# Forget block with heads in pairs, decay rows added by VectorE, and attention half steps between the products; projection after the gate in the PLE blocks

## What is computed

```python
def fox_mixer(hn, w_in, b_f, g_qn, g_kn, w_o):
    z = hn @ w_in                      # q, k, v: 16 heads of 64 each, and 16 forget logits
    log_f = jax.nn.log_sigmoid(f_logit + b_f)
    decay = jnp.cumsum(log_f, axis=1)
    q = rms_norm(q, g_qn)
    k = rms_norm(k, g_kn)
    # softmax over s <= t of q.k / 8 + decay[t] - decay[s], times v
    o = block_causal_attention(q, k, v, decay)
    return o.reshape(b, s, hd) @ w_o
# PLE, at the end of each layer
gate = jax.nn.sigmoid(rms_norm(h, g_ple[i]) @ ple_w_gate[i])
h = h + gate * (p[i] @ ple_w_proj[i])
```

## Time and profile before

| what | value |
|---|---|
| median of three runs | 1390.44 us |
| the profiled execution, own time | 1387.38 us |
| its span | 1385.6 us |
| TensorE busy | 1342.7 us, 97% |
| VectorE busy | 796.2 us, 57% |
| ScalarE busy | 676.5 us, 49% |

### The profile page before, as it was taken

How to read it: one execution, slowest core, us unless ns; L and a number is a source line. 1 busy time by engine, 2 the same in 40 slices (tenths; PEclk the granted TensorE clock), 3 DMA queues, 4 the chain that set the end, 5 groups by cost and what they waited for, 6 DMA issues and landing times.

```text
span 1385.6 us, 17642 instructions
## 1 busy us (share of the span) xinstructions
PE 1342.7 (97%) x6539; PEld 1110.8 (80%) x6539; DVE 796.2 (57%) x1008; ACT 676.5 (49%) x949; POOL 145.9 (11%) x206
## 2 busy tenths in 40 slices
PE   8999998899999999999999999999999899999996
PEld 6888787778888887888888878888888687888875
DVE  6655548784555546655545566555554645654664
ACT  6444336655444437544435463544444635447441
POOL 1000003611000001000001400000000142110500
PEclk9999999899999999999999999999999999999999
DMA  9655535234655654555553442465564478544531
GB/s 302 197 183 188 193 138 158 87 108 152 200 186 189 213 182 153 180 184 182 195 188 135 162 142 70 130 197 188 183 213 152 152 201 262 160 145 159 188 138 31
DMA packets 148526, 234.35 MB, mean 169 GB/s; under 512 B 10103, under 2 KB 103447, under 8 KB 148208
## 3 DMA queue, kind: packets, MB, share of 16 engines
q1 hardware_dynamic: 143680, 222.52, 49.4%
q0 software_dynamic: 4480, 10.85, 2.7%
q10 hardware_dynamic: 304, 0.14, 0.0%
HBM read 231.33 MB, written 4.49 MB: 170 GB/s over the span
## 4 chain that ended last, share of the span: by engine, by line
PE 84%; DVE 6%; ACT 3%; DMA 3%; issue 2%; POOL 1%; SPq 0%; POOLq 0%; DVEq 0%; ACTq 0%
PE acc L541 17%; PE acc L543 17%; PE acc L542 16%; PE acc L574 9%; PE acc L575 8%; PE acc L578 8%; PE misc L616 4%; DMA raw<-in_w_in_dram 2%; DVE wl L1474 1%; ACT xh L1095 1%; ACT wh L1059 1%; DVE xl L1500 1%; PE acc L754 1%; DMA rstd_by_token<-rstd 1%; PE misc L771 1%
## 5 line engine op out<-in xcount | busy, mean ns | idle before, releaser
L1474 DVE TENSOR_TENSOR wl<-raw,wh 128x2048 fp32r<-128x2048 f32 (+2 forms) x206 | 466.1, 2269 | 266.8 <-ACT wh L1059 266.5
L1059 ACT ACTIVATE wh<-raw 128x2048 fp32r<-128x2048 f32 (+2 forms) x206 | 387.4, 1888 | 174.4 <-PE acc L578 152.9
L541 PE MATMUL acc<-wh,xh 128*128 128x512 f32 (+2 forms) x848 | 333.4, 393 | 5.3 <-DVE wl L1474 2.7
L543 PE MATMUL acc<-wh,xl 128*128 128x512 f32 (+2 forms) x848 | 328.3, 387 | 0.0
L542 PE MATMUL acc<-wl,xh 128*128 128x512 f32 (+2 forms) x848 | 327.9, 387 | 0.0
L541 PEld LDWEIGHTS acc<-wh,xh 128*128 128x128 f32 x848 | 160.2, 189 | 39.2 <-issue 4.3
L543 PEld LDWEIGHTS acc<-wh,xl 128*128 128x128 f32 x848 | 160.1, 189 | 32.9
L542 PEld LDWEIGHTS acc<-wl,xh 128*128 128x128 f32 x848 | 160.5, 189 | 30.6
L574 PE MATMUL acc<-wh,ah 128*128 128x512 f32 x320 | 125.7, 393 | 0.0
L575 PE MATMUL acc<-wl,ah 128*128 128x512 f32 x320 | 124.6, 389 | 0.0
L2063 POOL TENSOR_SCALAR rstd<-ssq 128x1 f32<-128x1 f32 x20 | 10.3, 516 | 928.1 <-ACT hn L1079 927.8
(11 more groups left out here) (298 smaller groups left out, 1712.4 us busy)
## 6 DMA issues: line engine op xcount, KB each, us to landing
raw<-in_ffn_w_in_dram SPq DMA_DIRECT2D x172, 512.0 KB, 4.7
raw<-in_ffn_w_out_dram SPq DMA_DIRECT2D x88, 512.0 KB, 4.4
raw<-in_w_in_dram SPq DMA_DIRECT2D x64, 512.0 KB, 4.8
raw<-in_fox_w_in_dram SPq DMA_DIRECT2D x24, 512.0 KB, 4.2
raw<-in_ple_w_gate_dram SPq DMA_DIRECT2D x16, 512.0 KB, 4.1
raw<-in_mla_w_o_dram SPq DMA_DIRECT2D x8, 512.0 KB, 4.0
raw<-in_fox_w_o_dram SPq DMA_DIRECT2D x8, 512.0 KB, 4.5
raw<-in_w_out_dram SPq DMA_DIRECT2D x8, 512.0 KB, 4.7
```

The costliest lines, as they stand in the source:

```text
L541: pe.matmul(dst, hi, rhs_h, start=first, stop=False)
L543: return pe.matmul(dst, lo, rhs_h, start=False, stop=last)
L1059: act.activation(wh[:, s, 0:n], raw[:, s, 0:n], ACT.Copy).then_inc(hi_done, 1)
L1474: dve.tensor_tensor(wl[:, s, 0:n], raw[:, s, 0:n], wh[:, s, 0:n].bitcast(F32), ALU.subtract)\
```

## The change

In the forget block:
- Heads go in eight pairs. q and k of a pair are turned together, without the extra columns; the scores of the two heads are products of 64 rows at partitions 0 and 64, in different banks.
- The decay isn't in the product any more. TensorE turns the negated sums to rows, GpSimd writes them to DRAM and reads them back for all partitions (`negc`, 2 MB), and adds the causal mask (`mask_decay`). VectorE adds them to the scores with tensor_tensor_reduce, which gives the maximum too.
- Chunks come in the order q, k, v, q, k, v, so pairs 0 to 3 are ready after half of the projection. The pipeline of a pair is in half steps (even: turn q and k, products with v of two pairs before, turn the result, which ScalarE rounds and VectorE takes the remainder of; odd: scores, turn the probabilities of the pair before). Half steps 0 to 8 stand behind half groups of the projection (`FOX_AT`), the others between the products of the output matrix (`o_rows`), which begin as soon as a pair's result is turned.
- ScalarE and VectorE follow the same order; each now copies one lane of the turned probabilities.

In the PLE blocks the gate comes first and the projection after it; `pp` is gone, VectorE multiplies the gate by the accumulator; before the last block the roundings alternate between the token tiles and both squares stand behind them. Its core:

```diff
+PAIRS = H // 2
+FOX_CHUNKS = [0, 2, 4, 1, 3, 5]
+FOX_TURN = {4: (0, 1), 5: (2,), 6: (3,), 7: (4,), 8: (5,), 9: (6,), 10: (7,)}
+FOX_AT = {(7, 1): (0,), (8, 0): (1,), (8, 1): (2,), (9, 0): (3,), (9, 1): (4,), (10, 0): (5,), (10, 1): (6,),
+          (11, 0): (7,), (12, 1): (8,)}
+FOX_REST = 9
...
-                wide(g, I["ple_w_proj"][i], 0)
                 for k in range(4):
-                    wide(g + 1 + k, I["ple_w_gate"][i], 256 * k)
+                    wide(g + k, I["ple_w_gate"][i], 256 * k)
+                wide(g + 4, I["ple_w_proj"][i], 0)
...
+                def gate_wait(t, k):
+                    if t == 0 and k == DK - 2:
+                        rows_ready(pe, r, 1)
+                        turn_rows(nname, 1)
+                    ready(t, k)
+                wide_stage(g, q, xh, xl, DK, 0, gate_wait, None, True)
...
+                    for n in range(2):
+                        open_tile(q + 2 + n, t)
+                        for k in range(2):
+                            if t + n + k == 3:
+                                turn_h(after, r_after)()
+                            mm = products(acc(q + 2 + n, t), ph[:, k, t * P:(t + 1) * P], pl[:, k, t * P:(t + 1) * P],
+                                          wh[:, s, w], wl[:, s, w], k == 0, k == 1)
+                        mm.then_inc(acc_ready if t == 0 else (proj_ready, w_used)[n], 1)
...
+            def even(i):
+                if i < PAIRS:
+                    fill = q + fox_fill(1 if i < PAIRS // 2 else 4)
+                    if i % (PAIRS // 2) == 0:
+                        pe.wait_ge(acc_read[fill % 2], acc_reads(fill))
+                    for b, src in enumerate((qf, kf)):
+                        open_m(b, hr[b] + 2 * i)
+                        for t in range(NT):
+                            mm = turn(b, slice(t * P, (t + 1) * P), src[:, t, i * P:(i + 1) * P])
+                        mm.then_inc(m_ready[b], 1)
+                j = i - 2
+                if 0 <= j < PAIRS:
+                    fill = q + fox_fill(2 if j < PAIRS // 2 else 5)
+                    if j % (PAIRS // 2) == 0:
+                        pe.wait_ge(acc_read[fill % 2], acc_reads(fill))
+                    pe.wait_ge(m_read[2], hr[2] + 2 * j + 1)
+                    pe.wait_ge(m_read[3], hr[3] + probs_at(j) + 1)
+                    for lane in range(2):
+                        v = vf[:, :, (2 * j + lane) * HD:(2 * j + lane + 1) * HD]
+                        for t, blocks in enumerate((((0, 0),), ((1, 0), (2, 1)))):
+                            for n, (col, kt) in enumerate(blocks):
+                                mm = pe.matmul(M[:, 2, t * P + lane * HD:t * P + (lane + 1) * HD],
+                                               pTf[:, lane, col * P:(col + 1) * P], v[:, kt, :],
+                                               start=n == 0, stop=n == len(blocks) - 1)
+                    mm.then_inc(m_ready[2], 1)
+                if i in FOX_TURN:
+                    open_m(3, hr[3] + turned_at(i))
+                    for n, j in enumerate(FOX_TURN[i]):
+                        pe.wait_ge(m_read[2], hr[2] + 2 * j + 2)
+                        for t in range(NT):
+                            mm = turn(3, slice(n * S + t * P, n * S + (t + 1) * P), hn[:, t, j * P:(j + 1) * P])
+                    mm.then_inc(m_ready[3], 1)
+            def odd(i):
+                if i < PAIRS:
+                    for b in range(2):
+                        pe.wait_ge(m_read[b], hr[b] + 2 * i + 1)
+                    for t, w in enumerate((P, S)):
+                        for lane in range(2):
+                            rows = slice(lane * HD, (lane + 1) * HD)
+                            mm = pe.matmul(M[:, lane, t * P:t * P + w], qTf[rows, t * P:(t + 1) * P], kTf[rows, 0:w],
+                                           start=True, stop=True)
+                            if t:
+                                mm.then_inc(m_ready[lane], 1)
+                j = i - 1
+                if 0 <= j < PAIRS:
+                    for lane in range(2):
+                        pe.wait_ge(fox_exp, 2 * j + lane + 1)
+                        open_m(2 + lane, hr[2 + lane] + (2 * j, probs_at(j))[lane])
+                        for n in range(3):
+                            mm = turn(2 + lane, slice(n * P, (n + 1) * P), prf[:, j % 2, lane, n * P:(n + 1) * P])
+                        mm.then_inc(m_ready[2 + lane], 1)
...
+            for n in range(1, 6):
+                fill = q + fox_fill(n)
+                open_acc(fill)
                 for k in range(2):
...
+                    w = fox_group(n) + k
+                    wait_group(g + w)
+                    for half in range(2):
+                        for j in range(2 * half, 2 * half + 2):
+                            for t in range(NT):
+                                cols, wc = slice(t * P, (t + 1) * P), slice(512 * j, 512 * j + 512)
+                                mm = products(acc(fill, t), xh[:, 4 * k + j, cols], xl[:, 4 * k + j, cols],
+                                              wh[:, (g + w) % RING, wc], wl[:, (g + w) % RING, wc],
+                                              k + j == 0, k == 1 and j == 3)
+                                if t == 0 and k == 1 and j == 3:
+                                    mm.then_inc(acc_ready, 1)
+                        if half:
+                            mm.then_inc(w_used, 1)
+                        attend((w, half))
...
+            def o_rows(j, t):
+                s = (g + 13 + j // 2) % RING
+                if t == 0 or j < 5:
+                    wait_group(g + 13 + j // 2)
+                    e = min(i for i in FOX_TURN if j in FOX_TURN[i])
+                    pe.wait_ge(m_read[3], hr[3] + turned_at(e) + 1)
+                for n in range(2):
+                    if j == 0:
+                        open_tile(q + 7 + n, t)
+                    w = slice((j % 2) * D + n * 512, (j % 2) * D + (n + 1) * 512)
+                    mm = products(acc(q + 7 + n, t), xh[:, j, t * P:(t + 1) * P], xl[:, j, t * P:(t + 1) * P],
+                                  wh[:, s, w], wl[:, s, w], j == 0, j == DK - 1)
+                    if j == DK - 1 and t == 0:
+                        mm.then_inc(acc_ready, 1)
+                if t == NT - 1 and j % 2:
+                    mm.then_inc(w_used, 1)
+            for n in range(FOX_REST, 2 * PAIRS + 3):
+                (odd if n % 2 else even)(n // 2)
+                if n >= 10:
+                    o_rows((n - 10) // 2, (n - 10) % 2)
+            o_rows(4, 1)
+            o_rows(5, 0)
+            even(PAIRS + 2)
+            o_rows(6, 0)
+            o_rows(7, 0)
+            for j in (5, 6, 7):
+                if j == 7:
+                    turn_h("n6", 6)()
+                o_rows(j, 1)
...
+            def odd(i):
+                j = i - 1
+                if 0 <= j < PAIRS:
+                    act.wait_ge(m_ready[3], hf[3] + probs_at(j) + 1)
+                    act.activation(pTf[:, 1, :], M[:, 3, 0:3 * P], ACT.Copy).then_inc(m_read[3], 1)
+                if i < PAIRS:
+                    for lane in range(2):
+                        act.wait_ge(fox_max, 2 * i + lane + 1)
+                        for t, (a, b) in enumerate(((0, P), (P, 3 * P))):
+                            part = prf[:, i % 2, lane, a:b]
+                            e = act.activation(part, part, ACT.Exp, bias=nmx[:, t, 2 * i + lane:2 * i + lane + 1],
+                                               accum_out=rs[:, t, 2 * i + lane:2 * i + lane + 1])
+                        e.then_inc(fox_exp, 1)
...
+            def matrix_out(g, q, r, nname):
+                residual(q, g + 3, 1.0, 0)
+                split_to(g + 6)
                 rest(nname, r, 0)
...
+                residual(q, g + 3, 1.0, 1)
                 split_to(done[0] + 1)
                 rest(nname, r, 1)
...
+                def embed(t, n):
+                    fill = q + 2 + n
+                    if t == 0:
+                        dve.wait_ge(acc_ready, fill + 1)
+                    elif n == 0:
+                        dve.wait_ge(proj_ready, 1 if name == "p0" else 2)
+                    else:
+                        dve.wait_ge(w_used, g + 5)
+                    dve.wait_ge(acc_read[(q + n) % 2], acc_reads(q + n))
+                    cols = slice(512 * n, 512 * n + 512)
+                    dve.tensor_tensor(gate[:, t, cols], acc(fill, t), gate[:, t, cols], ALU.mult)\
+                       .then_inc(acc_read[fill % 2], 1)
+                    dve.wait_ge(acc_read[fill % 2], acc_reads(fill) - 1 + t)
+                    e = dve.tensor_tensor(h[:, t, cols], h[:, t, cols], gate[:, t, cols], ALU.add)
+                    if n:
+                        e.then_inc(h_added, 1)
                 split_to(g + 7)
...
+                embed(0, 0)
+                embed(0, 1)
+                embed(1, 0)
+                if after == "n8":
+                    embed(1, 1)
```

(89 more changed lines are left out.)

429 lines of the change are left out of this document (207 added, 222 removed).

## The result

The changed kernel takes 1395.05 us (median of 16 runs, 1391.26 to 1397.66), the kernel before 1388.57 (16 runs): ratio 1.0041, 95% interval 1.0034 to 1.0049, so slower by 5.7 us by the ratio; the medians lie 6.5 us apart. I had forecast 1389.0 and no change that can be told. (The forecast was added to the 1390.44 of three runs; sixteen runs put the kernel before at 1388.57.)

A forecast was written before the change was run, and what follows sets the result against it. TensorE, busy 1342.7 of 1385.6 us, was taken as the bound. From 1387.4, forget block +0.8 and PLE blocks -1.0 and -1.2 gave 1386.0; with 3.0 added, 1389.0 us, range 1378.5 to 1397.5.

The forecast's parts named there:

- TensorE's work: Forget block: a pair of heads takes 3.54 us instead of 4.52; with holes included, 16.0 us would go.
- idle of the earlier trace that goes: Forget block, start and end of the old pipeline: TensorE's 4.3 us of idle go, within the 16.0.
- group 7: Projection: weights ready 12.4 us after chunk n=1's end, TensorE comes after 11; wait 1.5 us, 0 to 3.
- half step 4: In group 9: banks wait for VectorE's sum, scaling and split before half step 3's maxima; 4.9 us idle in all.
- half steps 8 and 9: Wait behind chunk n=4 costs nothing at half step 8; TensorE waits 0.2 us for kT at 9.
- half steps 10, 12, 15, 16: Tail: TensorE waits for VectorE and ScalarE, with splits in the way: 1.8, 2.2, 2.3 and 0.5 us.
- norm: After the output products: waits of 1.3 and some 0.4 us at the two tiles replace 0.79; 0.9 us.
- clock at half step 4: Behind the 3.8 us hole the clock falls to half speed for 6.8 us, losing 3.4 us; 0 if it doesn't.
- clock in the tail: Half steps 12 and 15: main forecast charged no clock loss; a rival put up to 6.8 us there.
- the PLE blocks: Projection moved behind the gate: gains of 1.0 us at the first such block and 1.2 at the second.
- the new wait at the third chunk: Last block: a new hole of nearly 5 us at its third chunk, released by the read of u.
- the clock falls in the tail as well: Rival: holes at half steps 12 and 15 cost up to 3.4 us each, 6.8 together, so 1395.8; chance 0.19.

The follow-up runs named there:

- kernel with quarters: Changed kernel with scaling behind the maxima, inverse norms ahead of the broadcast, and splits of groups 15 and 16 moved, group 15's remainder in quarters: 1377.42 us (0.9918).
- block of 80 transposes: Kernel before, with 80 useless transposes in one block ahead of chunk 4's first group in the forget block's projection: 1397.63 us (1.0054).

## Why the prediction was wrong

By its own steps; the measured value is from the profile of the changed kernel.

| step | forecast | measured |
|---|---|---|
| TensorE's work (the 16.0 without the 4.3 of idle in it) | -11.7 | -7.9 |
| idle of the earlier trace rows that goes | -4.3 | -4.3 |
| group 7 | 1.5 | 1.7 |
| half step 4 | 4.9 | 3.6 |
| half steps 8 and 9 | 0.2 | 3.9 |
| half steps 10, 12, 15, 16 | 6.8 | 3.5 |
| norm | 0.9 | 0.8 |
| half step 1 | 0 | 0.3 |
| clock at half step 4 | 3.4 | 3.3 |
| clock in the tail | 0 | 3.4 |
| clock at the logits | 0 | -1.6 |
| forget block, the terms added | +1.7 | +6.9 |

(The measured column adds to 6.7; the 0.2 are rounding.) The forecast's terms add to +1.7, not to the +0.8 on record: 16.0 - 1.5 - 4.9 - 7.0 - 0.9 - 3.4 is -1.7. Added rightly they give 1389.9. So this slip is 0.9 of the miss, and the steps below are the rest.

*Right:* the mechanism of group 7 and half step 4, each confirmed by an edit that removed it, and their size to 1.3 us (half step 4 was 3.6 and not 4.9; group 7's 1.7 is in part luck, since six profiles with this wait show 0.6 to 1.7); the clock fall there; the PLE blocks in sum, as far as the noise tells (1.9 by the medians, 1.3 by the profiles, of 2.2); the new wait at the third chunk. I had the last released by u. The row says VectorE's split, which stands in line behind u (u from 1134.72, the split from 1136.05, TensorE at 1138.48). What I took over as fixed ahead of u was not: the two small reads of the inverse norm (`rstdp`, 0.5 KB) land after 2.3 to 3.2 us in the four profiles with the old PLE blocks, and after 2.9 to 6.8 in the nine with the new ones, where the DMA engines are busier with weights at that time (in the changed kernel 363 GB/s from 1131 to 1132, in the kernel before 35 from 1122 to 1123). That the weights are the cause is not tested.

*The first step that failed* was TensorE's work, by 3.8 us. I had named the new kernel's busy time a sum of durations between starts. The sum was nearly good (3.67 a pair against 3.54, 1.0 for eight), but by two errors that cancel. I had read the earlier trace rows as 1.25 us; the next product begins at 1151.97, so the eight records took 1.07, which makes 0.80 by columns, and 0.85 was measured for my 1.0:

```profile
1151.97 0.50 PE L541 MATMUL acc<-wh,zh 128*128 128x512 f32 x1
```

Against that, the two runs of six products in a pair take 1.57 and 1.47 in the loop, not 1.36. What was missing is the cost of stopping. A short wait costs some 0.2 us more than its row names (1.98 against 1.30 over three waits), a long one under 0.1 (the run of six products ahead of half step 15 takes 3.85 in place of 1.57, and its row names 2.22). Over the 11 waits of the changed kernel ahead of its norm that is some 1.9 by the rows. This is worked out from rows, not tested by itself, and 0.9 stays open. It also means that removing long waits gives back none of this work: in the kernel with quarters, whose waits are all short, TensorE's work over the same products is within 0.3 us of the changed kernel's.

*The second* was "the same wait behind chunk n=4 costs nothing, since half step 8 comes only after four half groups". The maxima had that time, but what follows them in ScalarE's and VectorE's order (exponentials, the split of group 14, the key) had not; and the mask pass, which I charged only with its own lateness, slowed VectorE by 3.1 us (1.6 on the split, 1.5 on the negation) just there. Together 3.7 us more than I had at half steps 8 and 9, and 1.7 of clock. Without the mask pass 1.3 us of the wait were left, so the claim would have failed without it too.

*The third* was the clock of the tail. I gave the rival "the clock falls in the tail as well" 0.19, at 1395.8, and the time came out there. That agreement is largely luck. Only half of its 6.8 us is that mechanism: the falls cost 1.7 each, not 3.4, and one of them stood at half step 9, where I saw no hole. The other errors made up the rest. The waits of half steps 10, 12 and 16 were smaller than forecast. Behind the fall at half step 9 there is none at 10, likely because TensorE comes late at half clock, while the kernels without that fall show two or three short ones there; but even those add to 0.75 at most for my 1.8, half step 12 has 1.3 for 2.2, and half step 16 none in any kernel with the splits in their old place. I had priced VectorE too high, with 0.9 us a lane of maxima, which take 0.74 (794.96 to 795.70, from one lane's start to the next).

The rule of the Trainium skill (TensorE: Matmul & The Clock Gate, section Part 4: PE-mode transpose) that I had set beside that rival finds no support in the block of 80 transposes: 1.00 throughout its 8.65 us.

## What to carry over

When work is put between products, write down for every queue what stands ahead of the operation that frees the next bank, and follow it on through the second engine: a wait for a third engine (here GpSimd's norms) ahead of it costs more than its own length. The same edit was a loss of 0.4% or part of a gain of 1.2%, by the order of some ten instructions on VectorE, ScalarE and GpSimd alone. Background work that waits for another engine goes where the next input is far; here it also went in pieces, which was not tried apart.

## What I had not expected of the hardware

- How much a GpSimd pass over 1024 elements a partition costs VectorE: splits of 2.28 us took up to 4.48, and an operation of 0.17 took 1.69. Both engines lose: GpSimd's second pass took 4.45 beside a split.
- Whether a hole lowers the granted clock is partly chance. The hole of 3.3 us at half step 4 was followed by a fall in all four profiles that have it, that of 2.2 us at half step 15 in five of six, the 1.56 us before the last block in three of nine, and the three short waits of half step 12 (0.7, 0.3 and 0.3) in two of six. Over the MLA block, with one and the same code, between 1.7 and 10.2 us were lost. So a hole should be priced with a share of 1.7 to 3.4 us, and one profiled execution is several us uncertain by this alone.
